# Second block's output projection, done row tile by row tile with attention's half of the inner dimension first

## Chip, cores and metric

The kernel runs on one core of a Trainium2 chip. The metric is the device time of one execution in microseconds (us), a median over runs.

## What is computed

A token sequence of 256 rows and 1024 columns goes through two copies of a first block and then through one second block. The change is in the mixer of the second block. Of the reference, this matters:

```python
def _rms(x):
    x32 = x.astype(jnp.float32)
    return (x32 * lax.rsqrt(jnp.mean(x32 * x32, -1, keepdims=True) + EPS)).astype(x.dtype)

def _sgu(u, v, ln_g, w_s, b_s):
    u = jax.nn.gelu(u)
    v = _layernorm(jax.nn.gelu(v), ln_g)
    ...
    return u * mixed.reshape(bsz, length, SGU_W)

def _merge(o_na, o_sgu, out_gain, w_out):
    y = jnp.concatenate([_rms(o_na), _rms(o_sgu)], axis=-1) * out_gain
    return y @ w_out

        o_na = _neighborhood_attention(q, k, v, kc, vc, rpb[i])
        o_sg = _sgu(u, vs, sgu_ln[i], sgu_w[i], sgu_b[i])
        x = x + g_a[:, None] * _merge(o_na, o_sg, out_gain[i], w_out[i])
        hf = _modulate(x, sh_f[:, None], sc_f[:, None])
        x = x + g_f[:, None] * _hier_moe(hf, rg_w[i], rg_b[i], re_w[i], re_b[i], w1[i], w3[i], w2[i])
```

So the input `y` of the projection with `w_out` (1024 x 1024) has two halves of 512 columns: the first comes from attention (8 heads), the second from the gate (`gelu(u)` times a mixed `v`). Each half of each row has its own root-mean-square norm. After the projection, a residual sum, another such norm and a router with 16 experts follow.

## The kernel before

Rows are held in two row tiles of 128 (t = 0 and 1). Five engine programs (PE, ACT, DVE, POOL and SP, which loads weights) are each written as one Python function; each walks through the same plan of weights with a `Walk` object `W`, and each engine executes its instructions strictly in the order in which its function issues them. Every wait is a semaphore count.

Every fp32 product is made of three matmuls (`mm3`, lines 843 to 845): the stationary and the moving operand are each split into a high and a low part (`h` and `l`). Weights come as units of 512 x 512: one DMA into `raw`, then two ACT copies (L1611, into `whs`) and two DVE subtractions (L2253, into `wls`), each for half a unit. There are three slots for split units; a slot is free for another unit when its last matmul is done. `W.release` marks that and, unless `W.slow` or `W.hold` is set, `pump` splits the next units at once; `W.feed(n)` splits n halves at a stated point.

Around the change the program runs thus:

- `attention2` is a list of steps i = 0 to 20 that run beside the last matmuls of the input projection. Step i takes item i - 3 (one of 16 pairs of row tile and head) through the transpose `turn2` (four 128 x 128 transposes on PE into bank 7, one ACT copy out of it) and item i - 5 through `weigh2` (8 small matmuls in the page's rows, L1390). What else runs is in the table `beside`: step 16 has `gate_u` (ACT: gelu of `u`, out of banks 2 and 3), step 17 `gate_out` (DVE: product with `vb`; ACT: its squares), and one and two steps later DVE computes the sum's root (`rms_eps`, POOL, `rms`).
- `y_columns(t, g, b)` brings half g of row tile t of `y` into the layout for matmuls: four transposes on PE into bank b; a scale by `ogain` in four pieces (by ACT for g = 0, by DVE for g = 1, `to_affine`); an ACT copy into `P0h`; a DVE subtraction into `P0l`. I call these y00, y01 (row tile 0, gate), y10 (row tile 1, attention) and y11.
- The projection is two `gemm_rows`. A group is 12 matmuls: four inner pieces of 128, three matmuls each, 512 columns. The first call does column half 0 with `seq=((0, 0), (1, 0), (1, 1), (0, 1))` (inner half, row tile), so that y10 is wanted last, in the fourth group; y10's transposes stand in the third. The second call does column half 1, row tile 0 and then row tile 1.
- `merged2` (DVE) takes each finished quarter (column half c, row tile t) from its bank: product with the gate row, sum into `h`, statistics (`bn_stats`); after the second quarter of a row tile also the norm's factor (POOL) and the scaled rows `xs_f`. `f_columns` transposes those for the router and the experts; those of row tile 0 stand inside the last group, those of row tile 1 after it.

In `profile` rows `memT` holds attention's rows (`ona`), `end` the gate's rows (`ub`, `vb`), `mid` and `arena` the scaled pieces, `P0h`/`P0l` the two parts of `y`.

## Time and profile before

| | |
|---|---|
| median of 3 runs | 1578.8 us (1578.11 to 1579.7) |
| profiled execution, its own time | 1578.79 us |
| its span | 1576.9 us |
| PE busy | 1538.0 us (98%) |
| DVE busy | 1167.1 us (74%) |
| ACT busy | 919.9 us (58%) |
| mean granted PE clock | 0.992 of full |

The span runs from the first to the last instruction of the profiled execution; the 1.9 us between it and the time lie around it. Busy shares are means over a program with many stages, so they don't say what the stage of the change waits for.

### The profile page before, as it was taken

To read this page: it belongs to the slowest core of one execution; us is meant where nothing else is said; L and a number is where in the kernel's file an instruction comes from. 1 tells how busy PE (TensorE), PEld (TensorE's weight loads), DVE (VectorE), ACT (ScalarE), POOL (GpSimd) and SP (SyncE) were. 2 spreads that over 40 slices of the span, in tenths; PEclk is the share of its full clock that TensorE was granted. 3 is DMA by queue.
4 is the path that set the end of the run, shared out by engine and by line. 5 is a ranking of instruction groups with operands and counts; after the bars stand their busy time and mean duration, and the time that the engine had idled before them with its cause. 6 is when DMAs were issued, how large, how long until landed. Compare 5 with 4: busy or idle time off the path is not lost.

```text
span 1576.9 us, 20278 instructions
## 1 busy us (share of the span) xinstructions
PE 1538.0 (98%) x8024; PEld 1288.4 (82%) x8024; DVE 1167.1 (74%) x1628; ACT 919.9 (58%) x1421; POOL 82.6 (5%) x75
## 2 busy tenths in 40 slices
PE   9999999999999999999999999999989889999997
PEld 9988888888888798889888788888857778878785
DVE  7458857667885673687576579877665689999998
ACT  5468644655444444875447554443455468888884
POOL 0010000000000000100000000000200000000005
PEclk9999999999999999999999999999999999999999
DMA  7535335437675453543455358983431239999994
GB/s 287 206 134 213 134 117 213 157 129 284 249 266 214 150 190 142 200 182 126 160 187 187 133 216 321 343 320 139 182 127 54 112 132 373 368 379 373 371 369 167
DMA packets 52201, 339.35 MB, mean 215 GB/s; under 512 B 7835, under 2 KB 8477, under 8 KB 13316
## 3 DMA queue, kind: packets, MB, share of 16 engines
q1 hardware_dynamic: 48932, 331.79, 56.4%
q0 software_dynamic: 3168, 6.20, 1.1%
q8 instruction: 65, 1.06, 0.3%
q14 instruction: 36, 0.29, 0.1%
HBM read 332.82 MB, written 10.49 MB: 218 GB/s over the span
## 4 chain that ended last, share of the span: by engine, by line
PE 85%; DVE 8%; ACT 3%; issue 1%; POOL 1%; DMA 1%; SPq 0%; DVEq 0%; ACTq 0%; POOLq 0%
PE bank L843 25%; PE bank L845 24%; PE bank L844 24%; PE bank L849 4%; DVE wls L2253 3%; PE bank L1002 2%; PE bank L1130 1%; POOL sm L3210 1%; PE bank L1191 1%; PE bank L1169 1%; DMA raw<-in_ws_dram 1%; PE bank L1110 1%; ACT whs L1611 1%; DVE sm L2235 1%; DVE h L2223 1%
## 5 line engine op out<-in xcount | busy, mean ns | idle before, releaser
L2253 DVE TENSOR_TENSOR wls<-raw,whs 128x1024 fp32r<-128x1024 f32 x426 | 507.1, 1226 | 172.4 <-ACT whs L1611 171.6
L1611 ACT ACTIVATE whs<-raw 128x1024 fp32r<-128x1024 f32 x426 | 429.3, 1051 | 208.7 <-PE bank L845 167.0
L843 PE MATMUL bank<-whs,P1h 128*128 128x512 f32 (+1 forms) x732 | 290.5, 397 | 2.1 <-issue 2.1
L845 PE MATMUL bank<-whs,P1l 128*128 128x512 f32 (+1 forms) x732 | 284.4, 389 | 0.0
L844 PE MATMUL bank<-wls,P1h 128*128 128x512 f32 (+1 forms) x732 | 283.7, 388 | 0.0
L843 PE MATMUL bank<-whs,P0h 128*128 128x512 f32 (+1 forms) x640 | 257.4, 402 | 4.0 <-DVE wls L2253 2.6
L845 PE MATMUL bank<-whs,P0l 128*128 128x512 f32 (+1 forms) x640 | 249.8, 390 | 0.0
L844 PE MATMUL bank<-wls,P0h 128*128 128x512 f32 (+1 forms) x640 | 249.4, 390 | 0.0
L843 PEld LDWEIGHTS bank<-whs,P1h 128*128 128x128 f32 x732 | 137.6, 188 | 29.5 <-issue 3.0
L845 PEld LDWEIGHTS bank<-whs,P1l 128*128 128x128 f32 x732 | 137.5, 188 | 29.0
L844 PEld LDWEIGHTS bank<-wls,P1h 128*128 128x128 f32 x732 | 137.8, 188 | 26.6
L843 PEld LDWEIGHTS bank<-whs,P0h 128*128 128x128 f32 x640 | 121.7, 190 | 31.5 <-issue 3.5
L845 PEld LDWEIGHTS bank<-whs,P0l 128*128 128x128 f32 x640 | 121.3, 190 | 25.8
L844 PEld LDWEIGHTS bank<-wls,P0h 128*128 128x128 f32 x640 | 121.7, 190 | 23.7 <-issue 0.7
L1595 ACT ACTIVATE arena<-bank 128x256 f32<-128x256 f32 (+2 forms) x147 | 69.4, 478 | 87.1 <-PE bank L845 55.9
L3210 POOL TENSOR_TENSOR sm<-sm,mhalf 128x1 f32<-128x1 f32 (+1 forms) x30 | 26.5, 884 | 1004.5 <-DVE sm L2227 893.7
L1597 ACT ACTIVATE arena<-arena,sm 128x128 f32<-128x128 f32 (+2 forms) x80 | 40.1, 502 | 61.4 <-DVE sm L2227 61.3
L849 PE MATMUL bank<-ident,arena 128*128 128x128 f32 x410 | 64.4, 276 | 6.9 <-ACT arena L1595 5.1
L2253 DVE TENSOR_TENSOR wls<-landing,whs 128x1024 fp32r<-128x1024 f32 x56 | 66.4, 1220 | 2.1 <-ACT whs L1611 1.6
L849 PEld LDWEIGHTS bank<-ident,arena 128*128 128x128 f32 x410 | 50.7, 146 | 18.5 <-ACT arena L1595 6.3
L1611 ACT ACTIVATE whs<-landing 128x1024 fp32r<-128x1024 f32 x56 | 56.8, 1054 | 4.4 <-PE bank L845 4.4
L843 PE MATMUL bank<-P0h,whs 128*128 128x256 f32 x192 | 55.2, 288 | 1.1 <-DVE wls L2253 1.1
(300 smaller groups left out, 2509.4 us busy)
## 6 DMA issues: line engine op xcount, KB each, us to landing
raw<-in_ws_dram SPq DMA_DIRECT2D x264, 1024.0 KB, 4.8
landing<-in_ws_dram SPq DMA_DIRECT2D x38, 1024.0 KB, 7.0
lnb<-in_ln_g_dram SPq DMA_DIRECT2D x6, 512.0 KB, 5.7
lnb<-in_ln_b_dram SPq DMA_DIRECT2D x6, 512.0 KB, 6.8
ydram<-arena POOLq DMA_DIRECT2D x4, 512.0 KB, 8.4
mid<-in_bias_dram SPq DMA_DIRECT2D x1, 2048.0 KB, 9.8
h<-in_x_dram SPq DMA_DIRECT2D x2, 512.0 KB, 4.0
lnb<-in_mem_dram SPq DMA_DIRECT2D x1, 1024.0 KB, 12.5
```

Source lines behind the costliest of these rows:

```text
L843: e.matmul(out, x[0], w[0], start=start, stop=False, skip_group_check=skip)
L844: e.matmul(out, x[0], w[1], start=False, stop=False, skip_group_check=skip)
L845: return e.matmul(out, x[1], w[0], start=False, stop=stop, skip_group_check=skip)
L849: return e.transpose(out, in_, ident[0:n, 0:n])
L1002: m = e.matmul(banks[b][:, ct * 256:ct * 256 + 256], w[:, 2 * b4 + k, ct * 128:(ct + 1) * 128], xc[:, 2 * b4 + k, :], start=k == 0, stop=k ...
L1110: m = e.matmul(banks[4 + o][:, j * w:(j + 1) * w], qT[p:p + 64, hd // 2, t * 128:(t + 1) * 128], kT[p:p + 64, hd // 8, 0:w], start=True, s ...
L1130: m = e.matmul(banks[6][:, (hd % 8) * 64:(hd % 8 + 1) * 64], PTb[i % 2][:, j * (t + 1) + k, :], qkv[:, k, 1152 + 64 * (hd // 8):1216 + 64 ...
L1595: e.activation(out, in_, func, bias=bias, scale=scale).then_inc(*act.done(*key))
L1597: e.activation(out, in_, func, bias=bias, scale=scale, accum_out=acc).then_inc(*act.done(*key))
L1611: e.activation(hi, src, ACT.Copy, bias=0.0, scale=1.0).then_inc(*high.done(n, f))
L2253: e.tensor_tensor(lo, src, f32(hi), ALU.subtract).then_inc(*low.done(n, f))
L3210: e.tensor_tensor(out, in_, mhalf[:, 0:in_.shape[1]], ALU.pow).then_inc(*pool.done(*key))
```

## The change

Three things change, in all engine programs alike.

1. The units of `w_out_2` are loaded in the order (inner half 0, column half 0), (0, 1), (1, 0), (1, 1). They are called u0 to u3.
2. The projection is one `gemm_tiles` with the sequence `MIX_SEQ` of (unit, row tile): attention's half of row tile 0 for both column halves (u0, u1), then u2 for row tile 0, then u0 and u1 for row tile 1, u3 for row tile 0, u2 and u3 for row tile 1. The finished quarters come after the groups 3, 6, 7 and 8; before, after 2, 4, 6 and 8.
3. `gate_u` moves from step 16 to step 18, behind y00, and `gate_out` to step 19 on ACT and step 18 on DVE. `y_columns` for y01 and y11 leave step 20 and stand with y10 behind the first two groups (`gated`). They use banks 7, 5 and 4, and the scratch `sq_y` in `arena`.

```diff
-    for c in range(2):
-        wide("w_out_2", 0, c * 512)
+    by_rows("w_out_2", 0)
...
+        MIX_SEQ = ((0, 0), (1, 0), (2, 0), (0, 1), (1, 1), (3, 0), (2, 1), (3, 1))
...
-            W.gemm_rows("w_out_2", 2, seq=((0, 0), (1, 0), (1, 1), (0, 1)), mid=lambda: y_columns(1, 0, 5),
-                        part=rows_part(("mo", 0), PA, y2_ready, lambda t: t, lambda t: ((vec, "mo", t, 0),)))
-            W.slow = True
-
-            def merged2(t):
-                if t:
-                    W.slow, W.hold = False, True
-            W.gemm_rows("w_out_2", 2, by_src=True, mid=lambda: f_columns(0, True), evac=merged2,
-                        part=rows_part(("mo", 1), PA, y2_ready, lambda t: 2 + t, lambda t: ((vec, "mo", t, 1),)))
+            W.gemm_tiles("w_out_2", MIX_SEQ, OUT_AT[0], tiles_part(
+                ("mo",), PA, y2_ready, OUT_AT, lambda c, t: 2 * c + t, lambda c, t: (vec, "mo", t, c)),
+                at={(1, 4): gated, (4, 4): hold, (6, 4): lambda: W.feed(1), (7, 1): lambda: f_columns(0, True)})
...
-            beside = {2: [(gelu_v,)], 16: [(gate_u, 0), (gate_u, 1)], 17: [(gate_out, 0), (gate_out, 1)],
-                      18: [(y_columns, 0, 0, 4, "ph2")], 20: [(y_columns, 0, 1, 2, "ph2"), (y_columns, 1, 1, 3, "ph2")]}
+            beside = {2: [(gelu_v,)], 18: [(y_columns, 0, 0, 4, "ph2"), (gate_u, 0), (gate_u, 1)],
+                      19: [(gate_out, 0), (gate_out, 1)]}
+
+            def gated():
+                y_columns(0, 1, 7, "merge", sq_y)
+                y_columns(1, 1, 5, "merge", sq_y)
+                y_columns(1, 0, 4, "merge", sq_y)
+
+            def hold():
+                W.hold = True
...
-                      17: [(gate_out, 0), (gate_out, 1)], 18: [(y_columns, 0, 0, 4, "ph2")],
-                      20: [(y_columns, 0, 1, 2, "ph2"), (y_columns, 1, 1, 3, "ph2")]}
+                      18: [(y_columns, 0, 0, 4, "ph2"), (gate_out, 0), (gate_out, 1)]}
```

How the order of instructions changes shows best at three places. The first is ACT at the end of attention, before the change. `arena<-bank7` is the copy of a `turn2`, `end<-bank2` and `end<-bank3` are the two gelus, `arena,sm<-end` the gate's squares, `mid2<-bank4` and `P0h<-mid2` the first of them y00.

```order
L1595 ACTIVATE arena<-bank7 128x512
L1595 ACT_TABLE_LOAD
L1595 ACTIVATE end<-bank2 128x512
L1595 ACTIVATE end<-bank3 128x512
L1595 ACTIVATE arena<-bank7 128x512
L1597 ACTIVATE arena,sm<-end 128x512 x2
L1595 ACTIVATE arena<-bank7 128x512
L1595 ACTIVATE mid2<-bank4,vec 128x128 x4
L1595 ACTIVATE P0h<-mid2 128x4x128
L1597 ACTIVATE arena,sm<-memT 128x512
```

And the same place of ACT in the changed kernel.

```order
L1596 ACTIVATE arena<-bank7 128x512 x3
L1596 ACTIVATE mid2<-bank4,vec 128x128 x4
L1596 ACTIVATE P0h<-mid2 128x4x128
L1596 ACT_TABLE_LOAD
L1596 ACTIVATE end<-bank2 128x512
L1596 ACTIVATE end<-bank3 128x512
L1598 ACTIVATE arena,sm<-end 128x512 x2
L1598 ACTIVATE arena,sm<-memT 128x512
L1596 ACTIVATE P0h<-arena 128x4x128 x2
L1596 ACTIVATE arena<-bank4,vec 128x128 x4
L1596 ACTIVATE P0h<-arena 128x4x128
```

The last two of the copies and y00 now come ahead of the table load, the gelus and the gate's squares; y10's four pieces (`bank4,vec`) come behind the copies of y01 and y11.

The second place is DVE right behind attention's last maximum, before the change: `end<-end` are the gate's products, `end<-end,sm` their norm, `memT<-bank6,sm` and `memT<-memT,sm` attention's row tile 1 and its norm.

```order
L2223 TENSOR_TENSOR end<-end 128x512 x2
L2229 TENSOR_SCALAR sm<-sm 128x1 x2
L2223 TENSOR_TENSOR P0l<-mid2,P0h 128x4x128
L2227 TENSOR_SCALAR end<-end,sm 128x512 x2
L2241 RECIPROCAL sm<-sm 128x8
L2223 TENSOR_TENSOR memT<-bank6,sm 128x512
L2229 TENSOR_SCALAR mid2<-bank2,vec 128x128 x4
L2223 TENSOR_TENSOR P0l<-mid2,P0h 128x4x128
L2229 TENSOR_SCALAR mid2<-bank3,vec 128x128 x4
L2223 TENSOR_TENSOR P0l<-mid2,P0h 128x4x128
L2229 TENSOR_SCALAR sm<-sm 128x1
L2227 TENSOR_SCALAR memT<-memT,sm 128x512
```

And in the changed kernel.

```order
L2226 TENSOR_TENSOR P0l<-mid2,P0h 128x4x128
L2226 TENSOR_TENSOR end<-end 128x512 x2
L2232 TENSOR_SCALAR sm<-sm 128x1 x2
L2230 TENSOR_SCALAR end<-end,sm 128x512 x2
L2244 RECIPROCAL sm<-sm 128x8
L2226 TENSOR_TENSOR memT<-bank6,sm 128x512
L2232 TENSOR_SCALAR sm<-sm 128x1
L2230 TENSOR_SCALAR memT<-memT,sm 128x512
L2232 TENSOR_SCALAR arena<-bank7,vec 128x128 x4
L2226 TENSOR_TENSOR P0l<-arena,P0h 128x4x128
L2232 TENSOR_SCALAR arena<-bank5,vec 128x128 x4
L2226 TENSOR_TENSOR P0l<-arena,P0h 128x4x128 x2
```

y00's subtraction moved ahead of the gate; the norm of attention's row tile 1 moved ahead of y01 and y11, which now wait behind it.

The third place is DVE at the end of the projection, from y10's subtraction on, before the change (banks 0 and 2 are row tile 0, banks 1 and 3 row tile 1; `wls` is the split of half a unit of weights).

```order
L2253 TENSOR_TENSOR wls<-raw,whs 128x1024 x2
L2223 TENSOR_TENSOR arena<-bank1,lnb 128x512
...
L2253 TENSOR_TENSOR wls<-raw,whs 128x1024 x2
L2223 TENSOR_TENSOR arena<-bank2,lnb 128x512
...
L2227 TENSOR_SCALAR arena<-h,sm 128x1024
L2253 TENSOR_TENSOR wls<-raw,whs 128x1024
L2223 TENSOR_TENSOR arena<-bank3,lnb 128x512
```

And in the changed kernel.

```order
L2256 TENSOR_TENSOR wls<-raw,whs 128x1024 x4
L2226 TENSOR_TENSOR arena<-bank2,lnb 128x512
...
L2230 TENSOR_SCALAR arena<-h,sm 128x1024
L2226 TENSOR_TENSOR arena<-bank1,lnb 128x512
L2226 TENSOR_TENSOR h<-h,arena 128x512
L2958 BN_STATS sm<-h 128x6
L2256 TENSOR_TENSOR wls<-raw,whs 128x1024
L2226 TENSOR_TENSOR arena<-bank3,lnb 128x512
```

The quarter of bank 1 stood ahead of row tile 0's last quarter (bank 2) and now stands between that one and the last of all (bank 3). No instruction is added or taken away, and the rows of POOL and SP stand in the same order as before.

## Rows read from the trace of the kernel before

**Rows 1.** The page's first line.

```profile
span 1576.9 us, 20278 instructions
```

**Rows 2.** Windows: the stretch, then busy us (instructions) of PE, PEld, DVE, ACT, POOL.

```profile
1228.50:1255.20 26.70, 25.21 (x112) 20.31 (x112) 18.06 (x31) 10.49 (x19) 1.10 (x2) 0.95 0.44 165
1286.00:1556.00 270.00, 269.23 (x1196) 216.06 (x1197) 257.69 (x296) 234.41 (x314) 23.77 (x19) 1.00 0.95 358
```

**Rows 3.** Timeline of PE, end of attention: start, us, instruction, idle before and releaser.

```profile
1219.66 0.66 PE L849 MATMUL bank<-ident,arena 128*128 128x128 f32 x4
...
1222.54 0.65 PE L849 MATMUL bank<-ident,arena 128*128 128x128 f32 x4 [1.39 <-ACT arena L1595]
1223.04 0.60 PE L849 MATMUL bank<-ident,memT 128*128 128x128 f32 x4
1223.47 2.08 PE L1390 MATMUL bank<-tail,arena 128*128 128x64 f32 x16
1227.26 1.66 PE L849 MATMUL bank<-ident,end 128*128 128x128 f32 x8 [1.71 <-DVE end L2227]
1228.58 0.78 PE L843 MATMUL bank<-whs,P0h 128*128 128x512 f32 x1
```

**Rows 4.** Timeline of ACT, end of attention, and y10.

```profile
1219.62 1.28 ACT L1595 ACT_TABLE_LOAD   x1
1220.91 1.08 ACT L1595 ACTIVATE end<-bank 128x512 f32<-128x512 f32 x2
...
1223.18 0.63 ACT L1597 ACTIVATE arena<-end 128x512 f32<-128x512 f32 x1
...
1223.82 0.58 ACT L1595 ACTIVATE arena<-bank 128x512 f32<-128x512 f32 x1
...
1225.45 0.63 ACT L1595 ACTIVATE P0h<-mid 128x512 fp32r<-128x512 f32 x1
...
1237.29 1.14 ACT L1595 ACTIVATE arena<-bank,vec 128x128 f32<-128x128 f32 x4 [4.53 <-PE bank L849]
```

**Rows 5.** Timeline of DVE, from y00's subtraction to the last quarter.

```profile
1226.12 0.69 DVE L2223 TENSOR_TENSOR P0l<-mid,P0h 128x512 fp32r<-128x512 f32 x1 [2.02 <-ACT P0h L1595]
1226.72 0.88 DVE L2227 TENSOR_SCALAR end<-end,sm 128x512 f32<-128x512 f32 x2
...
1227.75 0.69 DVE L2223 TENSOR_TENSOR memT<-bank,sm 128x512 f32<-128x512 f32 x1
1228.36 1.12 DVE L2229 TENSOR_SCALAR mid<-bank,vec 128x128 f32<-128x128 f32 x4
1230.17 0.69 DVE L2223 TENSOR_TENSOR P0l<-mid,P0h 128x512 fp32r<-128x512 f32 x1 [0.70 <-ACT P0h L1595]
...
1234.21 0.49 DVE L2227 TENSOR_SCALAR memT<-memT,sm 128x512 f32<-128x512 f32 x1 [0.66 <-POOL sm L3210]
...
1248.37 0.69 DVE L2223 TENSOR_TENSOR arena<-bank,lnb 128x512 f32<-128x512 f32 x1 [1.03 <-PE bank L845]
...
1251.87 0.75 DVE L2227 TENSOR_SCALAR arena<-h,sm 128x1024 f32<-128x1024 f32 x1 [0.66 <-POOL sm L3210]
1252.54 1.22 DVE L2253 TENSOR_TENSOR wls<-raw,whs 128x1024 fp32r<-128x1024 f32 x1
1255.21 0.69 DVE L2223 TENSOR_TENSOR arena<-bank,lnb 128x512 f32<-128x512 f32 x1 [1.45 <-PE bank L845]
```

**Rows 6.** Timeline of PE: groups 4 and 5, and `f_columns` of row tile 0.

```profile
1239.87 0.49 PE L843 MATMUL bank<-whs,P0h 128*128 128x512 f32 x1 [1.22 <-DVE P0l L2223]
...
1242.73 0.39 PE L843 MATMUL bank<-whs,P0h 128*128 128x512 f32 x1
...
1252.68 1.09 PE L849 MATMUL bank<-ident,arena 128*128 128x128 f32 x8 [0.27 <-DVE arena L2227]
```

**Rows 7.** Timeline of POOL: the norm's root of attention's row tile 1.

```profile
1233.63 0.55 POOL L3210 TENSOR_TENSOR sm<-sm,mhalf 128x1 f32<-128x1 f32 x1 [8.90 <-DVE sm L2229]
```

**Rows 8.** Windows, as rows 2; the third number from the end is the granted clock.

```profile
1228.50:1231.00 2.50, 2.50 (x8) 2.02 (x8) 1.70 (x6) 1.33 (x3) 0.00 (x0) 0.50 0.00 0
```

More of the change, by code:

```diff
@@ L2101, in scalar @@
             W.slow = False
-            W.gemm_rows("w_out_2", 2, seq=((0, 0), (1, 0), (1, 1), (0, 1)),
-                        mid=lambda: y_columns(1, 0, 5, "merge", sq_y))
-            W.slow = True
-            def merged2(t):
-                if t:
-                    W.slow, W.hold = False, True
-            W.gemm_rows("w_out_2", 2, by_src=True, mid=lambda: f_columns(0, True), evac=merged2)
+            W.gemm_tiles("w_out_2", MIX_SEQ, OUT_AT[0], at={
+                (1, 4): gated, (4, 4): hold, (6, 4): lambda: W.feed(1), (7, 1): lambda: f_columns(0, True)})
             f_columns(1, False)
@@ L2939, in merged2 @@
             def merged2(c, t):
-                s_, o = slice(c * 512, (c + 1) * 512), mo[2 * c + t]
+                s_, o = slice(c * 512, (c + 1) * 512), mo[3 if t else 2 * c]
                 ve.wait_ge(mm, "mo", c, t)
```

25 lines of the change are left out of this document (16 added, 9 removed).

## The prediction

> **What bounds the kernel now.** I read the page's head first, then windows by stage, then the timelines of PE, ACT, DVE and POOL around the projection. The execution has a span of 1576.9 us [rows 1]. In the expert stage behind the change, PE is busy for 269.23 of 270 us [rows 2], so it has no slack for anything that reaches it late: what delays the router delays the end by as much, and what brings it forward brings the end forward. Between attention's end and the router there are short waits, each for the chain over DVE and ACT. The reader should see four of them. PE waits 1.39 us for an ACT copy [rows 3], since ACT is busy with a table load of 1.28 us and two gelus in 1.08 us [rows 4]. It waits 1.71 us for the gate's norm [rows 3]. Its first matmuls run at half clock: 0.50 granted from 1228.5 to 1231 us [rows 8], that is 1.2 GHz, after the waits of 1.39 and 1.71 us. And group 4 waits 1.22 us for y10 [rows 6]. Behind that, groups 4 to 8 run closely, and DVE waits 1.45 us for the last quarter at 1255.21 us [rows 5]: there PE is the later one.
>
> **The change, part by part.** All times are on this trace's clock. No instruction is added or removed, and SP's and POOL's orders stay; so the sum consists of shifts alone.
>
> *Start of the projection.* With the table load and the gelus behind y00, the copy of item 14 follows its transposes (1219.66 + 0.66 [rows 3]), at 1220.35. Item 15's transposes follow at 1221.0 instead of 1222.54, and its copy at 1221.75 instead of 1223.82: 2.07 us earlier, with the gate's squares gone from ahead of it too. From that copy to y00's subtraction it was 1226.12 - 1223.82 = 2.30 us [rows 4, 5], all of it ACT work, so the subtraction runs from 1224.05 to 1224.75. Attention's last matmuls ended 1.15 us behind the start of the last copy (1223.47 + 2.08 - 1.15 = 1224.4; the last copy ends there, at 1223.82 + 0.58), so they now end near 1223.5 and are no obstacle. The first group starts at 1224.8 instead of 1228.58: 3.8 us earlier. A group takes 1242.73 - 1239.87 = 2.86 us after a wait [rows 6], else about 2.73; both attention groups end at 1230.3 at full clock.
>
> *The gate's chain.* It now begins when ACT has made `P0h` of y00, at 1225.45 + 0.63 - 2.07 = 1224.0 [rows 4]. Table load 1.28, gelus of 0.54 each: 1225.3 to 1226.4. DVE's products of about 0.65 us run from 1225.95 to 1227.25, the second square from 1227.45. A square and its read take 0.75, then DVE's small step, POOL's root (0.55 [rows 7]) and back: 0.8 from DVE's step to the norm. So the gate's second norm starts at 1229.05, against 1227.2 before. Then, in DVE's order, attention's row tile 1 leaves its bank (0.59 behind one norm, by 1227.75 - 1226.72 less one of the two 0.44 [rows 5]): 1229.65. Its square, step and root give its norm at 1229.65 + 0.75 + 0.75 + 0.81 = 1231.96, ended 1232.45. That is 2.2 us before the 1234.21 of now [rows 5].
>
> *y01, y11 and y10.* This is where the early start goes. DVE's pieces of y01 are queued behind that norm: they start at 1232.55 (1228.36 before). From the pieces to the subtraction it is 1230.17 - 1228.36 = 1.81 us, and 0.69 for it [rows 5]: 1235.07. Group 3 can't start before 1235.1; PE, done with 24 matmuls at 1230.3, has only 12 transposes (some 1.7 us) until then and stands idle for the other 3. The same buffer then takes y11: pieces at 1235.2, ACT's copy ends at 1236.95. Only then, in ACT's order, come y10's pieces, at 1237.0. From there to the first matmul on y10 it was 1239.87 - 1237.29 = 2.58 us [rows 4, 6]: group 4 starts at 1239.6. Before it was 1239.87. So the projection's start comes 3.8 us earlier, and its fourth group 0.3 us.
>
> *The end of the projection.* Five groups and row tile 0's `f_columns` remain in both kernels; PE alone would keep the 0.3 us. But row tile 1's first quarter, which DVE took after group 4, now closes after group 7. Group 6 starts at 1239.6 + 2.86 + 2.73 = 1245.2. About 0.25 us later ACT begins to split the unit that takes u1's slot, DVE follows 1.1 us behind with two halves of 1.2: free at 1248.95, where the quarter of bank 2 is due (1248.37 before [rows 5]). From it to the scaled rows it takes 1251.87 + 0.75 - 1248.37 = 4.25: 1253.2. Now the moved quarter: three instructions with starts 0.72 apart, 2.15 us, to 1255.35. Then half a unit of weights, 1.22 [rows 5], to 1256.6. Then the last quarter at 1256.6, against 1255.21. PE is no longer what is waited for: `f_columns` at 1253.25 (1252.68 before), and its last matmul is then some 0.6 us later than before, at 1255.8. What is queued behind that quarter on DVE are row tile 1's norm, its `f_columns`, the router, and the experts. The loss there is 1256.6 - 1255.2 = **+1.4 us**.
>
> *What a page would make of it.* The table load of 1.28 us was followed by the gelu after 0.01 us, at 1220.91, and began 0.01 us behind a copy [rows 4]. The Trainium skill, "ScalarE: Activation LUTs", What ACT_TABLE_LOAD costs, adds a drain of about 1.38 us to the load of 1.28. By the page's 2.66, with the drain all new in the gate's chain, the sum would be 1.4 us higher, at 1581.5; the trace shows no such drain where the load stands now, so I go by the row.
>
> *Sum.* 1578.79 us is the profiled execution's own time, 0.01 below the median of the runs. 1578.8 + 1.35 = **1580.1 us**, or +0.09%. A measurement of this kernel can hardly tell less than 0.2% (3.2 us) from no change, so the forecast is "within 0.2%".
>
> *Bounds.* The trace doesn't show how closely the new chain links up; 20 hand-overs of ACT, DVE and POOL with perhaps 0.05 us each are 1 us either way in group 4's start. DVE's tail can't gain more than the 1.4 us if it is not the last: then 1578.5. Upwards the clock is the unknown, below.
>
> **Rivals.**
>
> *The early start is kept (faster).* The 3.8 us reach the end if y01 and y10 are there when PE wants them, at 1230.3 and 1233. With the 1.2 us that six matmuls at half clock cost (0.43 instead of 0.23 us each [rows 8]) and the 1.2 us wait for y10 gone, it could come to -4.3 us net of DVE's tail: 1574.5. For it: the first two groups really don't need the gate. Against it: DVE's order, in which y01 stands behind two norms, and the chain above that ends at 1235.1.
>
> *The low clock returns and lasts (slower).* Place: PE's idle time from 1231.4 to 1235.1 and before group 4. Now the half clock held for 3.5 us after waits of 1.39 and 1.71 us [rows 3, 8]; in the changed kernel some 3 us of idle time out of 4 stand in one stretch. Each matmul at 1.2 GHz costs 0.2 us more. Group 3 has 1.6 us of slack before y10 is there, which hides 8 of them; each further one is paid. It decides from 17 slow matmuls behind 1235.1 on (9 paid, 1.8 us, with the 1.4 above over 3.2). One stretch as long as now's, begun at the restart, is nearly hidden; a second one from group 4 on, 8 matmuls slow, gives +1.6, with group 3 slow to its end +0.7: in all +3.7, 1582.5. The Trainium skill, "TensorE: Matmul & The Clock Gate", Part 1, says that the throttled clock is the default and that activity releases it; that is the mechanism of this rival, and the trace agrees that the clock fell after waits and rose while matmuls ran.
>
> *DVE's tail isn't on the path (no change).* If PE or ACT decides, as they do at 1255.21 now, the time is 1578.5. Against it: 4.25 + 2.15 + 1.22 us of DVE work stand in a row behind group 6, and PE has only 5.5 + 0.9 us there. *A drain* of 1.4 us in the gate's chain gives 1581.5, still within 0.2%.
>
> **How the numbers follow.** Forecast, 1580.1 with its own range of 1579 to 1581.5: 0.64. DVE's tail hidden, 1578.5: 0.10. Drain or other loose hand-overs, 1581.5: 0.08. Low clock, 1582.5: 0.13, most of it slower by over 0.2%. Early start kept, 1574.5: 0.05. The range of 1577.9 to 1582.4 leaves out the early start and the worse half of the low clock, 0.13 or so. Faster 0.06, same 0.82, slower 0.12.
>
> **What would show it.** In the changed profile: first projection matmul 3.8 us earlier against attention's items; behind 24 matmuls, an idle stretch of over 3 us that ends with DVE's `P0l`; group 4 where it is now within 0.7 us; DVE without a wait between the quarters of banks 2, 1 and 3; `f_columns` of row tile 0 waiting over 1 us inside group 8. The prediction is wrong if the last quarter starts before 1255.2 or after 1258, or if the experts' 270 us change.

## The result, and the profile after

| | before | after |
|---|---|---|
| median of 20 runs each, us | 1577.49 (1576.52 to 1584.14) | 1581.41 (1579.51 to 1585.24) |
| ratio of the times, with its 95% interval | 1 | 1.0020 (1.0013 to 1.0026) |
| profiled execution's own time / its span, us | 1578.79 / 1576.9 | 1579.6 / 1577.8 |
| mean granted clock of that execution | 0.992 | 0.990 |

The ratio is a loss of 3.2 us (2.1 to 4.1); the quotient of the two medians would make it 3.9. The time lies inside the forecast's range and on the border of the 0.2% that counted as no change; the forecast was a loss of 1.35 us. Everything below sorts this into what the traces of the two orders show, and what the clock may have added.

The two traces can't be laid on each other by their own times. At attention's last group of scores, ahead of every instruction that the change moves, the changed kernel's trace is already 1.41 us earlier. That is chance: in the fourteen traces of this document the row stands anywhere from 1211.4 to 1215.3 us, on average at 1212.7 with the old order (four traces), 1212.8 with the changed one (seven) and 1213.0 with that of e8 (three). Here is the row in the timeline of PE of the kernel before.

```profile
1213.38 1.13 PE L1372 MATMUL bank<-tail,arena 64*128 64x512 f32 x4 [0.99 <-DVE arena L2227]
```

And here the timeline of PE of the changed kernel, from that row to `f_columns` of row tile 0 (start, us, instruction, idle time before it and what ended it).

```profile
1211.97 1.13 PE L1372 MATMUL bank<-tail,arena 64*128 64x512 f32 x4 [1.00 <-DVE arena L2230]
...
1223.45 0.47 PE L843 MATMUL bank<-whs,P0h 128*128 128x512 f32 x1 [1.03 <-DVE P0l L2226]
...
1231.28 0.66 PE L849 MATMUL bank<-ident,memT 128*128 128x128 f32 x4 [1.24 <-DVE memT L2230]
...
1233.99 0.47 PE L843 MATMUL bank<-whs,P0h 128*128 128x512 f32 x1 [2.06 <-DVE P0l L2226]
...
1234.99 0.63 PE L844 MATMUL bank<-wls,P0h 128*128 128x512 f32 x1
...
1238.40 0.39 PE L843 MATMUL bank<-whs,P0h 128*128 128x512 f32 x1
...
1251.78 1.09 PE L849 MATMUL bank<-ident,arena 128*128 128x128 f32 x8 [0.92 <-DVE arena L2230]
```

All distances from here on are counted from the start of a trace's own L1372 row. The first projection matmul stands at 1223.45 - 1211.97 = 11.48, against 1228.58 - 1213.38 = 15.20 [rows 3]: 3.7 us earlier, as forecast. Then PE waits twice, 1.24 us for attention's norm of row tile 1 and 2.06 us for y01. Group 4 starts at 1238.40, distance 26.43, against 26.49 before [rows 6]: of 3.7 us nothing is left. The matmul at 1234.99 takes 0.63 us, where it is 0.39 at full speed: the clock has fallen again. Group 4 carries no bracket: its data were there just before the slow group 3 ended.

The timeline of ACT of the changed kernel, same columns.

```profile
1221.95 0.63 ACT L1596 ACTIVATE P0h<-mid 128x512 fp32r<-128x512 f32 x1
1222.60 1.28 ACT L1596 ACT_TABLE_LOAD   x1
1223.89 1.09 ACT L1596 ACTIVATE end<-bank 128x512 f32<-128x512 f32 x2
...
1235.11 0.63 ACT L1596 ACTIVATE P0h<-arena 128x512 fp32r<-128x512 f32 x1 [1.99 <-DVE arena L2232]
1235.64 1.13 ACT L1596 ACTIVATE arena<-bank,vec 128x128 f32<-128x128 f32 x4
```

The table load stands behind y00's copy, as planned. The copy of y11 at 1235.11 had waited 1.99 us for DVE; y10's four pieces at 1235.64 stand behind it, although the transposes of row tile 1's attention had been in their bank since 1231.9 (the `memT` row of PE, 1231.28 + 0.66).

The timeline of DVE of the changed kernel, same columns.

```profile
1230.73 0.49 DVE L2230 TENSOR_SCALAR memT<-memT,sm 128x512 f32<-128x512 f32 x1 [0.66 <-POOL sm L3216]
1231.33 1.12 DVE L2232 TENSOR_SCALAR arena<-bank,vec 128x128 f32<-128x128 f32 x4
1233.15 0.69 DVE L2226 TENSOR_TENSOR P0l<-arena,P0h 128x512 fp32r<-128x512 f32 x1 [0.69 <-ACT P0h L1596]
...
1237.46 0.69 DVE L2226 TENSOR_TENSOR P0l<-arena,P0h 128x512 fp32r<-128x512 f32 x1 [1.00 <-ACT P0h L1596]
...
1247.48 0.68 DVE L2226 TENSOR_TENSOR arena<-bank,lnb 128x512 f32<-128x512 f32 x1
...
1250.97 0.75 DVE L2230 TENSOR_SCALAR arena<-h,sm 128x1024 f32<-128x1024 f32 x1 [0.67 <-POOL sm L3216]
1251.64 0.68 DVE L2226 TENSOR_TENSOR arena<-bank,lnb 128x512 f32<-128x512 f32 x1
...
1253.69 1.21 DVE L2256 TENSOR_TENSOR wls<-raw,whs 128x1024 fp32r<-128x1024 f32 x1
1254.82 0.68 DVE L2226 TENSOR_TENSOR arena<-bank,lnb 128x512 f32<-128x512 f32 x1
```

y01's pieces (1231.33) begin only behind the norm (1230.73), and y01's subtraction ends at 1233.84, where group 3 begins. In the tail, the quarters of bank 2 (1247.48), bank 1 (1251.64) and bank 3 (1254.82) have no bracket: DVE never waits for PE there, where before it waited 1.45 us for the last one [rows 5]. The last quarter stands at 42.85, against 41.83 before: 1.0 us later. From here on the loss is fixed, since the router and the experts are behind it: the first expert matmul is at 1285.54, distance 73.57, against 72.55.

The windows of the changed kernel (stretch, its length, busy us and instructions of PE, PEld, DVE, ACT, POOL, granted clock, DMA share, GB/s).

```profile
1234.80:1238.40 3.60, 3.60 (x10) 2.64 (x9) 1.66 (x4) 2.29 (x6) 0.00 (x0) 0.53 0.97 402
...
1286.00:1290.00 4.00, 4.00 (x13) 3.13 (x12) 2.85 (x4) 3.47 (x5) 0.00 (x0) 0.57 0.02 4
...
1285.50:1555.50 270.00, 269.18 (x1191) 216.42 (x1192) 256.82 (x295) 233.58 (x312) 23.20 (x18) 0.99 0.94 356
```

The granted clock is at the 1.2 GHz level in two places: over group 3, and once more just behind the first expert matmul. The expert stage is as full as before (269.18 of 270 us, [rows 2]), but from its first matmul to the span's end it takes 292.3 us against 291.0. That closes the account of the two traces: -1.41 before the change's place, +1.02 to the last quarter, +1.3 in the experts, +0.9 in all, which is the difference of the spans.

### The profile page after: what moved, and what is told of

It reads as the page before. It is cut to its first block, busy times and chain, and to the rows that moved or that the text cites. A ratio compares the mean times of both kernels' runs of the same rounds, so it can differ in the third digit from the quotient of the medians.

```text
span 1577.8 us, 20280 instructions
## 1 busy us (share of the span) xinstructions
PE 1540.6 (98%) x8024; PEld 1291.0 (82%) x8024; DVE 1167.7 (74%) x1628; ACT 921.3 (58%) x1421; POOL 82.6 (5%) x75
## 3 DMA queue, kind: packets, MB, share of 16 engines
q8 instruction: 65, 1.06, 0.3%
## 4 chain that ended last, share of the span: by engine, by line
PE 88%; DVE 7%; ACT 3%; issue 1%; DMA 1%; POOL 1%; SPq 0%; DVEq 0%; ACTq 0%; POOLq 0%
PE bank L843 25%; PE bank L845 25%; PE bank L844 25%; PE bank L849 4%; DVE wls L2256 2%; PE bank L1002 2%; PE bank L1130 1%; PE bank L1191 1%; PE bank L1169 1%; PE bank L1110 1%; DMA raw<-in_ws_dram 1%; ACT whs L1612 1%; POOL sm L3216 1%; DVE arena L2235 1%; DVE sm L2238 1%
## 5 line engine op out<-in xcount | busy, mean ns | idle before, releaser
L843 PE MATMUL bank<-P1h,whs 128*128 128x256 f32 x192 | 56.3, 293 | 0.0
```

Source lines behind the costliest of these rows:

```text
L843: e.matmul(out, x[0], w[0], start=start, stop=False, skip_group_check=skip)
```

## The experiments

The edits are shown shortened. `keep_up(b, n)` issues n fp32 matmuls of `allone` into a bank that nobody reads (PE's rows of L829, two rows for each); the kernel before already has such matmuls at other places. A table at the end of this section holds the distances of all traces. The ratios are those of each kernel to the kernel before on the same chip: e1 to e4 share one set of its runs (median 1578.69), e5 to e8 another (1578.41), e9 to e12 a third (1578.53).

### The two kernels again (e1, e2)

No edit: the kernel before and the changed kernel, word for word.

> The kernel before, unchanged, as a control and for a second map of the granted clock. All theories: no difference in time (within 0.1%). In its first trace the clock stood at half for about 3.4 us at 1227 to 1232 us and at none of the later stages up to 1572. If the falls of the clock come by chance (theory 2), they stand elsewhere or in another number here; if they belong to the program (rival), they stand at the same places.

> The changed kernel, unchanged. Theory 1 (DVE's tail at the end of the projection, with row tile 1's first quarter moved behind row tile 0's last): costs 1.0 us of the trace, which is what the last quarter lost against attention's items in the first trace. Theory 2: the rest of the measured 3.1 us is the clock, above all a fall at the first expert's matmuls (1286 to 1290 us in the changed kernel's trace, none in the one before), which costs up to 1.7 us. If it is tied to the change, it stands there again; if by chance, it is not. Time: 1.001 to 1.003 of before.

Before again: 1577.78 us, ratio 0.9997 (0.9988 to 1.0006). After again: 1580.64 us, ratio 1.0012 (1.0004 to 1.0021). The loss repeats, smaller: 1.9 us. The new trace of the changed kernel has another pattern of the clock. Its timeline of PE:

```profile
1212.56 1.13 PE L1372 MATMUL bank<-tail,arena 64*128 64x512 f32 x4 [0.99 <-DVE arena L2230]
...
1219.69 1.80 PE L1390 MATMUL bank<-tail,arena 128*128 128x64 f32 x8
...
1225.57 0.47 PE L843 MATMUL bank<-whs,P0h 128*128 128x512 f32 x1 [0.98 <-DVE P0l L2226]
```

And its windows.

```profile
1218.00:1222.00 4.00, 3.92 (x23) 3.79 (x23) 0.00 (x0) 1.39 (x4) 0.00 (x0) 0.62 0.02 4
...
1237.00:1240.00 3.00, 3.00 (x9) 2.33 (x9) 1.31 (x3) 2.29 (x6) 0.00 (x0) 0.59 1.03 431
```

Here the clock fell once in attention's tail: the projection begins at 13.01 instead of 11.48, and the last quarter comes at 44.36, 1.5 us later than in the first trace of the same program. The experts' fall is absent. For comparison, the windows of the kernel before again (e1), where the clock was low nearly throughout attention's tail:

```profile
1218.00:1229.00 11.00, 10.81 (x49) 10.40 (x50) 5.12 (x14) 7.78 (x17) 1.10 (x2) 0.54 0.00 0
```

Eleven microseconds at half clock, and yet its first projection matmul is at 15.80 against 15.20, and its last quarter at 41.58 against 41.83. In the old order PE's small matmuls of that stage stand beside the table load and the gelus, for which PE waits anyway. In the new order these are out of the way, and less than 4 us at half clock cost 1.5 us. (With the clock held in the old order, e11 below, the start is at 14.74 and the last quarter at 40.39: the eleven slow microseconds cost 1.1 to 1.2.) The stretch has lost the wait that covered a slow PE.

### y10 ahead of y11, and the clock held (e3, e5, e9)

The step under test is "y10's pieces stand behind y11's copy". e3, on the changed kernel, in `gated` of all engines:

```diff
     y_columns(0, 1, 7)
-    y_columns(1, 1, 5)
     y_columns(1, 0, 4)
+    y_columns(1, 1, 5)
```

> The changed kernel with y10 ahead of y11 (transposes on PE and pieces on ACT and DVE). Theory of the prediction (the serial order y01, y11, y10 sets group 4): y10 is ready some 2.5 us earlier, at about 1.7 us behind the start of group 3, so that group 4 follows group 3 without a wait. With the clock at full that gains 1.7 us; with the clock at half through group 3, as in the changed kernel's trace, group 3 lasts 4.4 us and hides it: gain 0.2 us. Rival (PE's order or the split of weights sets group 4): no change in either case.

1581.27 us, ratio 1.0015 (1.0006 to 1.0025). The trace moved by 1.6 us: last quarter at 41.25 (changed kernel 42.85), first expert matmul at 71.97. Its timeline of PE has the wait for y01 as the last one of the projection's start; group 4 follows without a bracket.

```profile
1234.59 0.66 PE L849 MATMUL bank<-ident,memT 128*128 128x128 f32 x4 [1.68 <-DVE memT L2230]
...
1237.30 0.47 PE L843 MATMUL bank<-whs,P0h 128*128 128x512 f32 x1 [1.62 <-DVE P0l L2226]
```

This trace has no clock fall from 1200 to 1300 us, by chance, as e5 was to test: e3 with matmuls in the gaps.

```diff
     y_columns(0, 1, 7)
+    keep_up(6, 4)
     y_columns(1, 0, 4)
     y_columns(1, 1, 5)
+    keep_up(6, 8)
```

> The kernel of e3 (y10 ahead of y11), with 12 extra fp32 matmuls of 128 columns in PE's idle time around the transposes ahead of group 3, into a bank that isn't read. Stretches are counted from attention's last score matmuls (L1372): to DVE's last quarter it was 41.8 and 41.6 us in two traces of before, 42.9, 44.4 and 44.0 with the changed kernel's order, each with a fall of the clock over groups 3 and 4, and 41.25 in e3, without a fall. Theory (falls of the clock at group 3 follow from PE's idle time there): no fall between group 1 and the end of the projection, 41.2 us again, and the time 0.5 to 2 us below the changed kernel. Rival (the falls have nothing to do with that idle time): a fall can stand over groups 3 to 5 here too.

1579.70 us, ratio 1.0010 (1.0000 to 1.0020), last quarter at 41.27. So the order of y10 and y11 is worth 1.6 us in the traces and the matmuls in the gaps nothing; in the measured times neither is apart from the changed kernel, as the intervals overlap.

e9 is the changed kernel with the same matmuls in its own order.

```diff
     y_columns(0, 1, 7)
     y_columns(1, 1, 5)
+    keep_up(6, 4)
     y_columns(1, 0, 4)
+    keep_up(6, 8)
```

> The changed kernel with 12 extra fp32 matmuls of 128 columns (into a bank that isn't read) in PE's idle time around y10's transposes, ahead of group 3; the order y01, y11, y10 stays. In three traces with that order the clock fell over group 3 or 4 each time. Theory (PE's idle time there brings the falls, and the wait for y10 hides most of one): no fall over groups 3 to 5; group 4 still waits for y10, so the last quarter comes at 42.6 us behind the last scores (42.9, 44.4 and 44.0 with falls); time 0.3 to 1.5 us below the changed kernel. Rival (falls are set by something else): they stand there in spite of it.

1580.21 us, ratio 1.0012 (1.0003 to 1.0021), which is that of e2: the 0.3 to 1.5 us of gain that were expected aren't shown. Its timeline of PE:

```profile
1231.69 1.06 PE L829 MATMUL bank<-allone 128*128 128x128 f32 x8
...
1233.61 1.95 PE L829 MATMUL bank<-allone 128*128 128x128 f32 x16
1235.83 0.47 PE L843 MATMUL bank<-whs,P0h 128*128 128x512 f32 x1 [0.27 <-DVE P0l L2228]
...
1240.05 0.50 PE L843 MATMUL bank<-whs,P0h 128*128 128x512 f32 x1 [1.24 <-DVE P0l L2228]
```

The low clock over group 3 is gone, and what comes in its place is a wait of 1.24 us for y10 before group 4. The last quarter is at 42.80 against 42.85. Group 3 itself starts at the same distance, 22.02, in both. So the one fall over group 3 in the changed kernel's trace costs nothing, as the low-clock rival's working had it ("one stretch ... is nearly hidden"): DVE's chain through y01, y11 and y10 is what group 4 waits for.

### The fall at the experts (e4)

PE alone, behind the place where all expert rows are ready:

```diff
     mm.here("all_rows")
+    keep_up(0, 7)
```

> The changed kernel with 7 extra fp32 matmuls of 128 columns on PE, into a bank that isn't read, in the idle time of 2.0 us ahead of the first expert's matmuls. Theory 2 (the clock falls there since PE has waited): no fall of the clock at the first expert, up to 1.7 us faster than the changed kernel in the executions that have the fall, on average 0.5 to 1.5 us; ratio to before about 1.001. Rival (the fall there is an accident of one trace and the time lies in DVE's tail): same time as the changed kernel or up to 0.3 us slower.

1581.36 us, ratio 1.0015 (1.0005 to 1.0024). Windows:

```profile
1233.00:1239.00 6.00, 5.43 (x13) 4.35 (x14) 2.93 (x7) 2.29 (x6) 0.00 (x0) 0.50 0.85 354
...
1286.00:1290.00 4.00, 3.80 (x17) 3.16 (x18) 2.85 (x5) 3.09 (x5) 0.00 (x0) 1.00 0.01 4
```

No fall at the experts here, and the time did not improve. But e2 had none either without the edit, and e7, e9 and e11 have one. So that fall comes and goes from execution to execution in both orders (e11 is the old one), and nothing ties it to the change. This trace shows instead a longer stretch at half clock over groups 3 and 4, 6 us at 0.50, which shifted the last quarter to 43.95, 1.1 us behind the first trace: what the low-clock rival named as its second stretch.

### Each part alone (e6, e7)

e6, on the kernel before: only the gate later, with y01 and y11 left at step 20 and the projection in its old order.

```diff
-beside = {..., 16: [gate_u 0, gate_u 1], 17: [gate_out 0, gate_out 1], 18: [y00],
+beside = {..., 18: [y00, gate_u 0, gate_u 1], 19: [gate_out 0, gate_out 1],
           20: [y01, y11]}
```

> The kernel before, with only the third part of the change: gelus and gate rows behind y00. The order of the projection is the old one, so y01 and y11 are wanted before its first group. Theory (the prediction's chain): the gate's second norm comes 1.8 us later than before, counted from the last scores, so the first group starts about 2 us later (17.2 instead of 15.2) and everything behind it as well: last quarter at about 44, time +1.5 to +2.5 us. Rival (attention's tail is shorter and pays for it): first group where it was, no change.

1582.33 us, ratio 1.0025 (1.0016 to 1.0034). Timeline of PE:

```profile
1230.60 2.04 PE L849 MATMUL bank<-ident,end 128*128 128x128 f32 x8 [4.95 <-DVE end L2227]
1232.30 0.78 PE L843 MATMUL bank<-whs,P0h 128*128 128x512 f32 x1
```

PE stands 4.95 us for the gate's norm, since y01's and y11's transposes are queued ahead of the first group. First matmul at 18.68, 3.5 us later than before; last quarter at 44.87. Expected were 17.2 and about 44, and 1.5 to 2.5 us of loss, where 3.9 were measured. The direction is the theory's, the size is not. Two stretches of low clock lie in this trace's start (1220 to 1223 and 1227 to 1233), and the eight transposes took 2.04 us where e11, at full clock, has 1.09; how much of the surplus they make up wasn't tested.

e7, on the changed kernel: the gate back where it was, with the row tile order kept.

```diff
-beside = {..., 18: [y00, gate_u 0, gate_u 1], 19: [gate_out 0, gate_out 1]}
+beside = {..., 16: [gate_u 0, gate_u 1], 17: [gate_out 0, gate_out 1], 18: [y00]}
```

> The changed kernel without its third part: gelus at step 16 and gate rows at 17 again, ahead of y00; the projection's new order stays. Theory: first group at 15.2 us behind the last scores, as before (11.5 in the changed kernel), group 3 when y01 is made, which now waits for PE's transposes behind 24 matmuls: at about 24, against 22.0 in the changed kernel; last quarter some 2 us later than there, 45. Time +1.5 to +2.5 us against the changed kernel, +3.5 to +5 against before. Rival (the early start of the first two groups is worth nothing, since y01 waits for attention's norm and not for PE): same as the changed kernel.

1582.28 us, ratio 1.0026 (1.0016 to 1.0037). Timeline of PE:

```profile
1224.96 0.47 PE L843 MATMUL bank<-whs,P0h 128*128 128x512 f32 x1 [1.41 <-DVE P0l L2226]
...
1235.41 0.47 PE L843 MATMUL bank<-whs,P0h 128*128 128x512 f32 x1 [1.83 <-DVE P0l L2226]
```

And of DVE:

```profile
1228.05 0.49 DVE L2230 TENSOR_SCALAR memT<-memT,sm 128x512 f32<-128x512 f32 x1 [0.67 <-POOL sm L3216]
1232.75 1.13 DVE L2232 TENSOR_SCALAR arena<-bank,vec 128x128 f32<-128x128 f32 x4 [4.21 <-PE bank L849]
```

With the gate early and the new order, the start is at 13.58, 2.1 us later than in the changed kernel, and the last quarter at 44.80; the clock fell over group 1. The last quarter (45 expected), group 3 (24.03, 24 expected) and the time are as expected; the start isn't, at 15.2 expected. It is earlier than before because only y00 stands ahead of the first group here, while the kernel before also has y01's and y11's transposes there, which wait for the gate's norm [rows 3]. The wait before group 3 is still 1.83 us, and this run corrects my reading of it. Here attention's norm is long done (1228.05) when y01's pieces begin (1232.75): DVE waits 4.21 us for y01's transposes, which now stand in PE's queue behind the first two groups. So there are two queues in that wait. In the changed kernel the transposes were done at 1229.01 + 1.03 = 1230.04, and DVE took their result up at 1231.33: 1.3 us of the idle time there are the norm's. The other 2 are the chain from transposes over pieces, copy and subtraction to the matmul, for which PE has nothing else queued, and which an earlier norm would not remove. Each part alone loses about 4 us (0.25%), the two together 2 to 3, so the parts don't add up.

### Attention's half first for both row tiles (e8, e10, e12)

If order on DVE and ACT is what eats the start, it should pay to ask first for what is ready first. e8, on the changed kernel: all four groups of attention's half ahead of the gate's. y10's transposes then stand inside the second group, y01's at the end of the third and y11's inside the fourth; DVE makes attention's norm of row tile 1 ahead of the gate's products, and POOL its root ahead of the gate's; and the units take four slots, so that u3 is split ahead of the projection.

```diff
-MIX_SEQ = ((0,0),(1,0),(2,0),(0,1),(1,1),(3,0),(2,1),(3,1))
+MIX_SEQ = ((0,0),(1,0),(0,1),(1,1),(2,0),(3,0),(2,1),(3,1))
...
-W.open_slot(flat_pair(PB), first_of("w_out_2"))
+W.open_slot(flat_pair(PB), first_of("w_out_2") + 3)
...
-at={(1, 4): gated, (4, 4): hold, ...
+at={(1, 0): y10, then gate_out, (2, 3): y01, (2, 4): hold, (3, 1): y11, ...
```

> A version drawn from the theory: groups 1 to 4 are attention's half of both row tiles, groups 5 to 8 the gate's half. y10 comes ahead of the gate's norms on DVE, POOL and ACT, y01 behind it in group 3 and y11 in group 4; the fourth unit of weights is split before the projection, in a fourth slot that was kept free. Theory (the chain over y01 and y11 ahead of y10, then DVE's tail with two more splits in it, set the end): PE's groups follow each other from 11.5 us behind the last scores on with less than 2 us of waits, the last quarter comes at 38 to 39.5 instead of 41.8 (before) and 42.9 (changed): -2.5 to -3.5 us against before, -4 to -6 against the changed kernel. Rival (other work of DVE and ACT there is the bound): last quarter at 41 or later.

1578.55 us, ratio 1.0000 (0.9991 to 1.0009). Timeline of PE, then of DVE:

```profile
1212.17 1.13 PE L1372 MATMUL bank<-tail,arena 64*128 64x512 f32 x4 [0.99 <-DVE arena L2228]
...
1223.65 0.47 PE L843 MATMUL bank<-whs,P0h 128*128 128x512 f32 x1 [1.03 <-DVE sm L2242]
...
1230.46 0.50 PE L843 MATMUL bank<-whs,P0h 128*128 128x512 f32 x1 [0.54 <-DVE P0l L2224]
...
1247.78 1.09 PE L849 MATMUL bank<-ident,arena 128*128 128x128 f32 x8 [1.13 <-DVE arena L2228]
```

```profile
1243.50 0.67 DVE L2224 TENSOR_TENSOR arena<-bank,lnb 128x512 f32<-128x512 f32 x1
...
1247.64 0.68 DVE L2224 TENSOR_TENSOR arena<-bank,lnb 128x512 f32<-128x512 f32 x1
...
1250.82 0.68 DVE L2224 TENSOR_TENSOR arena<-bank,lnb 128x512 f32<-128x512 f32 x1
```

One wait of 0.54 us is left between the first group and `f_columns`, in place of 1.24 and 2.06. The last quarter is at 38.65, 3.2 us ahead of the kernel before and 4.2 ahead of the changed one; the first expert matmul at 69.37 (72.55, 73.57). DVE's tail is the same as in the changed kernel, without a wait for PE from bank 2's quarter to the end, only that it starts 4.2 us sooner. So the expectation is met in the trace (38 to 39.5) and missed in the time (-2.5 to -3.5 us against before). Run again (e12, no edit):

> The kernel of e8, unchanged, for more runs and a second trace. If its stage really is 3 us shorter and only falls of the clock vary, the ratio to before lies at 0.998 to 0.9995 and the stretch from the last scores to the last quarter is 38.65 us plus what a fall inside it costs. If the gain is lost behind that stage, experts' first matmul to the end is over 291.2 us.

1576.79 us, ratio 0.9994 (0.9985 to 1.0004), with the last quarter at 38.65 again. Two traces agree on a gain of 3 us to that point, and two measurements give 0.0 and 0.9 us. To ask whether the clock in runs without a trace eats the rest, e10 puts matmuls in the gaps of e8.

```diff
+beside: 15: keep_up(1, 4), 16: keep_up(1, 1), 20: keep_up(1, 4)
+at: (1, 4): keep_up(7, 2)
```

> The kernel of e8 with 11 extra fp32 matmuls of 128 columns in PE's idle time from step 15 of attention to group 3. e8's trace had no fall of the clock there, and its last quarter came at 38.65, 3.0 us ahead of before; but its median over 11 runs was that of before. Theory (in other executions of e8 the clock falls in attention's tail or the projection and takes the 3 us back): this one keeps the gain in most executions, 1 to 3 us below before. Rival (the gain of e8's stage is lost elsewhere): no faster than e8.

1576.16 us, ratio 0.9985 (0.9976 to 0.9994): 2.4 us faster than the kernel before, the only one of the twelve whose interval excludes no change on that side. It is faster than the changed kernel too, whose two intervals (from 1.0013 and from 1.0004 up) lie above its own, and so does that of e9 on the same chip (from 1.0003 up). Its last quarter is at 38.69, the same as without the added matmuls, so they cost nothing in the trace. e10 and e12 overlap, so by the times alone what the added matmuls bring isn't shown.

### The clock held in the old order (e11)

```diff
+beside: 15: keep_up(1, 4), 17: keep_up(1, 5), 20: keep_up(1, 6) ahead of y01
```

> The kernel before with 15 extra fp32 matmuls of 128 columns in PE's idle time of attention's tail (steps 15, 17 and 20). Before had a fall of the clock in attention's tail in both traces, one over the first six matmuls of the projection and one across it; in the projection that costs up to 1.2 us. Theory: no fall there, first group at 15.2 or less behind the last scores and at full clock, last quarter at 40.6 to 41.8, time 0 to 1 us below before. Rival: extra matmuls delay attention's items, +0.5 us or more.

1578.99 us, ratio 1.0003 (0.9994 to 1.0012). In its trace the clock is at full level from attention's tail to the router, and the last quarter at 40.39, 1.4 us better than before. Its timeline of PE shows why the low clock over the first groups was paid in full there, although a wait for y10 followed it [rows 6]:

```profile
1234.07 0.60 PE L849 MATMUL bank<-ident,memT 128*128 128x128 f32 x4
...
1237.29 0.50 PE L843 MATMUL bank<-whs,P0h 128*128 128x512 f32 x1 [1.23 <-DVE P0l L2224]
```

The transposes for y10 stand in PE's queue behind the first groups. Slow groups make y10 late by as much, and the wait of 1.2 us stays: group 4 is at 25.06 here and at 26.49 before. In the changed order y10 doesn't hang on group 3, and so a slow group 3 is free (e9). With the clock held in both, then, the new order is behind by 42.80 - 40.39 = 2.4 us, not by 1.0: the kernel before had a fall in both of its traces, which hid 1.2 to 1.4 us of the difference.

The clock fell in e11 behind the first expert matmul instead (windows):

```profile
1283.00:1287.00 4.00, 3.65 (x9) 2.92 (x10) 2.85 (x5) 2.95 (x4) 0.00 (x0) 0.57 0.02 4
```

From that matmul to the span's end e11 takes 1575.3 - 1283.35 = 291.95 us, where the ten traces without a fall there have 290.8 on average: the fall costs 1.2 us. Holding the clock in the old order alone isn't a gain that can be measured (the interval reaches from -0.9 to +1.9 us), so e10's gain is not that of its added matmuls alone.

### All traces in one table

Distances in us from each trace's L1372 row. "Trace says" is the last quarter's difference to the mean of before's two traces (41.70); "measured" is the ratio less one, times 1578.

| kernel | first wout | last quarter | expert 1 | clock fell at (1200 to 1300) | trace says | measured |
|---|---|---|---|---|---|---|
| before | 15.20 | 41.83 | 72.55 | 1227.6 | | |
| e1 before again | 15.80 | 41.58 | 72.30 | 1218 to 1229 | | -0.5 |
| after | 11.48 | 42.85 | 73.57 | 1234.8, 1286 | +1.1 | +3.2 |
| e2 after again | 13.01 | 44.36 | 75.07 | 1218, 1236 | +2.7 | +1.9 |
| e4 expert keep | 11.48 | 43.95 | 74.66 | 1232 to 1240 | +2.2 | +2.4 |
| e9 after keep | 11.48 | 42.80 | 73.52 | 1288 | +1.1 | +1.9 |
| e3 y10 second | 11.48 | 41.25 | 71.97 | none | -0.5 | +2.4 |
| e5 same, keep | 11.49 | 41.27 | 71.98 | none | -0.4 | +1.6 |
| e6 gate late only | 18.68 | 44.87 | 75.59 | 1220, 1227 to 1234 | +3.2 | +3.9 |
| e7 gate early | 13.58 | 44.80 | 75.51 | 1225, 1287 | +3.1 | +4.1 |
| e8 attention first | 11.48 | 38.65 | 69.37 | none | -3.1 | 0.0 |
| e12 same, again | 11.48 | 38.65 | 69.35 | none | -3.1 | -0.9 |
| e10 same, keep | 11.48 | 38.69 | 69.39 | none | -3.0 | -2.4 |
| e11 before keep | 14.74 | 40.39 | 71.12 | 1283 | -1.3 | +0.5 |

The last two columns rank the kernels roughly alike, with e3 as the clearest exception, and the interval of a measured value is about 1.4 us either way. Yet where the trace has no fall and no added matmuls (e3, e8, e12), the measured time is 2.2 to 3.1 us above what the trace says. A trace is one execution; that its clock held doesn't say that it does so in the others. And the yardstick itself has falls in it: against e11's 40.39, every value of the column "trace says" is 1.3 us higher, which brings most of them nearer to the measured ones (e8 -1.7, e3 +0.9, after +2.5) and a few away from them (e2 +4.0, e4 +3.6, e10 -1.7).

Every single run has a mean granted clock on record, not only those with a kept trace, and sorted by it the runs say what the fourteen traces can't. "Before" in this table are all runs of the kernel before beside e1 to e12, and e1; the bounds were chosen after seeing the figures.

| runs | number | clock 0.989 or less | clock 0.992 or more |
|---|---|---|---|
| before | 113 | 55, mean 1579.0 us | 36, mean 1577.6 us |
| changed order (after, e2, e4) | 42 | 23, mean 1582.0 us | 2, mean 1580.8 us |
| e9, changed order with added matmuls | 11 | 2, mean 1580.8 us | 5, mean 1579.5 us |
| e8 and e12 | 22 | 8, mean 1579.4 us | 8, mean 1575.5 us |
| e10, the same with added matmuls | 11 | 0 | 6, mean 1575.7 us |

Two things follow. The gain of e8's order is there in the runs whose clock held (1575.5 against 1577.6 us) and gone in those whose clock was low (1579.4 against 1579.0), and e10 has none of the low ones. The groups are small, but this fits an order that is 3 us ahead in its traces and level in its median: both of its traces come from the upper group (0.993 and 0.994). And the changed order seldom keeps its clock: 2 of 42 runs reach 0.992, where before it is 36 of 113 (much the same in each of the sets beside the experiments: 9 of 35, 11 of 33, 12 of 33), and with matmuls in the changed order's waits 5 of 11. So not every low clock is an accident of a trace; the changed order meets it more often. Where in those runs the clock was low, this figure doesn't say.

## Why the prediction was right, point by point

The time lies in the stated range, and the mechanism is the forecast's: the early start is lost in the queues ahead of group 4, and DVE's tail makes the end later. The size of the loss is not: 1.35 us were forecast, and 3.2 (2.1 to 4.1) measured. That the time itself is off by only 1.3 us is in part luck: the forecast started from 1578.8 us, the median of three runs of the kernel before, and its twenty runs have 1577.49. That the ratio of 1.0020 still counts as within 0.2% is luck as well.

**Start of the projection, 3.8 us earlier.** Right: 3.7 us (15.20 to 11.48). Table load and gelus stand behind y00's copy.

**The gate's chain and attention's norm.** Right: the norm of row tile 1 at 1230.73 is 18.76 from the last scores, and 1231.96 was forecast, 18.58.

**y01 behind that norm, group 3 at 1235.1.** Right: 22.02 against 21.7 forecast. PE's idle time there was forecast as some 3 us in one stretch; it is 1.24 + 2.06 = 3.3 in two, and only the second ends with `P0l`. The step named DVE's queue as the reason; that is 1.3 us of it, and the rest is the chain behind transposes that are asked for only after two groups (e7, where the norm is early and 1.83 us remain).

**y10 behind y11, group 4 0.3 us earlier.** Right in place, 0.06 instead of 0.27 earlier. e3 shows it as a cause in the traces: with the two exchanged, the last quarter comes 1.6 us sooner (1.5 with the clock held, e5 against e9). No time shows it.

**DVE's tail, +1.4 us.** Right in mechanism: no wait between the quarters of banks 2, 1 and 3, and `f_columns` at 39.81 waits 0.92 (forecast 39.87, over 1 us). Bank 2's quarter to the last one takes 1254.82 - 1247.48 = 7.34 us, where 4.25 + 2.15 + 1.22 = 7.62 was forecast. Against the trace that the forecast used, the last quarter is late by 1.0 us, not 1.4: 0.5 up to bank 2's quarter and 0.5 in the tail. The stated bounds for the last quarter, 1255.2 and 1258, held: it is at 1213.38 + 42.85 = 1256.2 on the forecast's clock.

**The early start kept.** It wasn't. The rival's own size doesn't come out of its terms either: 3.8, 1.2 and 1.2 us less 1.4 of DVE's tail are 4.8, not 4.3.

**The drain.** The Trainium skill, "ScalarE: Activation LUTs", What ACT_TABLE_LOAD costs, gives a total of 2.66 us. The moved load began 0.02 us behind the copy and took 1.28, and the gelu began 0.01 us later (1221.95 + 0.63, 1222.60, 1223.89): the trace doesn't agree, in either position.

**The low clock.** This is the term that was mis-sized, on both sides of the comparison.

The forecast took the kernel before with the fall that its trace had [rows 8] and priced the six slow matmuls at 1.2 us, but asked only whether an early start would win that back. It didn't ask what the kernel before would do without the fall. With the clock held the old order's last quarter comes 1.4 us sooner (e11) and the new one's at the same distance (e9), and the loss between them is 2.4 us, where the forecast had 1.35. All three traces of the old projection order without added matmuls (before, e1, e6) have such falls, at places that vary, so its usual execution seems to have one as well.

On the other side, the forecast gave the low clock's return no price in the sum, as one stretch at the restart would be hidden, and 0.13 to a second one. The first half is shown: e9 removes that stretch and nothing comes earlier. But the clock also fell over groups 3 and 4 in a row in e4, which costs 1.1 us, and where the forecast had not looked, in attention's tail in e2. There less than 4 us at half clock cost 1.5 in the new order, while 11 us of it cost 1.1 to 1.2 in the old (e1 against e11). The three traces of the changed order without added matmuls in this stage have their last quarter at 42.85, 44.36 and 43.95, mean 43.7, which is 2.0 us behind before's mean. So the traces give 2.0 us with the falls as they came and 2.4 with the clock held; the times of this order gave 1.9, 1.9, 2.4 and 3.2 us (e2, e9, e4, and the first measurement).

The Trainium skill, "TensorE: Matmul & The Clock Gate", Part 1, has the throttled clock as the default that activity releases; the rows agree as far as every fall here came after or between waits of PE and ended while matmuls ran. Which waits bring one about, the rows don't tell: the same program with the same waits had a fall in attention's tail in one execution and not in another (e2 and after). That the changed order's waits make one likelier fits the table of clock figures (2 of 42 runs at 0.992 or more, 5 of 11 with matmuls in the waits).

**What stays open.** The traces account for 2.0 to 2.4 us. The first measurement's 3.2 us is about 1 us more, but its interval begins at 2.1, and the four intervals of this order share 2.1 to 3.3 us; the surplus may be noise. That runs with a low clock make up the rest fits the changed order's clock figures and the slow halves of e8 and e12, but wasn't tested: a run has one clock figure for all its 1580 us. Which part of e8's edit brings its 4.2 us, the order or the fourth slot, wasn't taken apart either.

## What to carry to other kernels

Work that is moved to the front of PE's queue starts early only until its first operand that another engine makes in a fixed order: follow that operand back through the queues of DVE, ACT and PE itself before counting a gain, and let the consumer ask in the order in which the producers deliver (e8: the last quarter 4.2 us sooner than in the changed kernel, by order and one more weight slot together).

A finished quarter that is moved late costs its evacuation on the engine that closes the stage (DVE's tail, 7.34 us in place of 6.84).

When waits are taken out of a stage, what they covered becomes visible, here a slow PE clock. A wait behind slow work hides nothing when its own operand comes out of that work (e11). Compare traces from a common instruction ahead of the change, take a second trace before believing a microsecond, and sort the runs by their mean clock before calling a gain in a trace lost.

## What the runs showed of the hardware

- The granted clock of one program differs from execution to execution, at the same instructions. After: 0.53 at 1234.8 and 0.57 at 1286; e2, the same program: 0.62 at 1218 and 0.59 at 1237, and 1.00 at the experts. The price of such a stretch was 0 (e9 against after), 1.1 (e4) and 1.5 us (e2), as something else was or wasn't later there.
- Matmuls of 128x128 into an unread bank filled 3.0 us of waits (e9: 8 and 16 of them in 1.06 and 1.95 us, two rows for each fp32 matmul) and delayed the matmul behind them by nothing that the last quarter shows (42.80 against 42.85).
- In 22 runs of one program (e8 and e12) the mean granted clock lay between 0.987 and 0.994, and the time followed it: 1575.5 us on average in the eight runs at 0.992 or more, 1579.4 in the eight at 0.989 or less. In 113 runs of the kernel before, the same two groups are 1.4 us apart.
